# Block compression of a paged cache: four products per two blocks, or three

## The reference

```
def compress(kv, w1, w2, pe):
    c = kv[:, :n_chunk * CMP_STRIDE].reshape(B, n_chunk, CMP_STRIDE, 2, N_KV_HEADS, HEAD_DIM)
    lo = jnp.einsum('bnjchd,cjde->bnche', c, w1[:, :CMP_STRIDE])
    hi = jnp.einsum('bnjchd,cjde->bnche', c, w1[:, CMP_STRIDE:])
    pe_term = jnp.einsum('cjd,cjde->ce', pe, w1)
    pre = lo[:, :-1] + hi[:, 1:] + pe_term[:, None, :]
    return jnp.einsum('bnche,ced->bnchd', jax.nn.gelu(pre), w2)
```

## Time and profile before

| | us |
|---|---|
| median of 3 runs | 1815.0 (1814.69 to 1815.51) |
| the profiled execution | 1820.48 |
| its span | 1818.8 |
| granted clock of TensorE, mean | 0.992 |
| PE busy | 1761.8 (97%) |
| DVE busy | 1205.3 (66%) |
| POOL busy | 802.4 (44%) |
| ACT busy | 765.5 (42%) |
| DMA moved | 214.60 MB, mean 118 GB/s |

### The profile page before, as it was taken

One profiled execution on the slowest core, in us unless ns is written; L12 is line 12 of the kernel. 1 busy time (PEld: TensorE's weight loads), 2 busy tenths in 40 slices (PEclk: granted clock), 3 DMA queues, 4 the chain that ended last, 5 costly groups with the idle time before them and its releaser, 6 DMA issues.

```text
span 1818.8 us, 36969 instructions
## 1 busy us (share of the span) xinstructions
PE 1761.8 (97%) x14084; PEld 1641.3 (90%) x14084; DVE 1205.3 (66%) x1909; ACT 765.5 (42%) x1433; POOL 802.4 (44%) x763
## 2 busy tenths in 40 slices
PE   8999999999998999999999899999999999999998
PEld 7999998999995767676899899999999999999998
DVE  6789975675466676767746754554587879845535
ACT  5312333345345666666524333333343333314435
POOL 2203972224303434344444666656565555325531
PEclk9999999999998999999999999999999999999999
DMA  4321365446413444444313222323393732332214
GB/s 157 126 75 44 105 192 151 131 98 166 109 49 117 132 126 128 121 126 117 119 47 129 102 95 106 119 95 107 119 310 127 212 130 96 134 102 63 59 35 142
DMA packets 189983, 214.60 MB, mean 118 GB/s; under 512 B 23012, under 2 KB 152736, under 8 KB 189287
## 3 DMA queue, kind: packets, MB, share of 16 engines
q1 hardware_dynamic: 179357, 188.89, 33.8%
q0 software_dynamic: 7840, 21.25, 4.2%
q10 hardware_dynamic: 2610, 2.10, 0.4%
HBM read 181.22 MB, written 35.55 MB: 119 GB/s over the span
## 4 chain that ended last, share of the span: by engine, by line
PE 53%; DVE 8%; issue 3%; ACT 3%; POOL 2%; DMA 1%; ACTq 0%; SPq 0%; DVEq 0%; POOLq 0%
PE ps L2660 11%; PE ps L3043 7%; PE ps L2665 6%; PE ps L2420 4%; PE ps L3048 4%; PE ps L200 3%; PE ps L1827 3%; PE ps L1839 3%; PE ps L1815 3%; PE ps L3556 2%; PE ps L1866 2%; POOL S L1782 1%; PE ps L206 1%; DVE S L2076 1%; PE ps L3566 1%
## 5 line engine op out<-in xcount | busy, mean ns | idle before, releaser
L1782 POOL TENSOR_SCALAR S<-S,inv,gate_p 128x640 f32<-128x640 f32 (+7 forms) x186 | 124.3, 685 | 195.5 <-DVE inv L2086 195.5
L1166 DVE SCALAR_TENSOR_TENSOR y<-u,conv_w,y 128x1024 f32<-128x1024 f32 x120 | 156.5, 1350 | 1.2
L433 POOL DMA_DIRECT2D raw<-in_cache_cmp_kv_dram x124 | 77.8, 631 | 149.9 <-DVE relaid L1252 121.1
L1010 PE MATMUL ps_p<-Xhi,w1hi 128*128 128x256 f32 x544 | 139.3, 293 | 1.4 <-ACT Xhi L715 1.4
L3043 PE MATMUL ps<-dn_op_hi,dn_hi 128*128 128x264 f32 x672 | 136.6, 285 | 2.8 <-DVE dn_op_lo L3091 2.8
L3043 PE MATMUL ps<-dn_op_lo,dn_hi 128*128 128x264 f32 x672 | 135.7, 283 | 0.0
L1010 PE MATMUL ps_p<-Xlo,w1hi 128*128 128x256 f32 x544 | 132.8, 283 | 0.0
L1236 DVE TENSOR_TENSOR Xlo<-ps_p,Xhi 128x512 fp32r<-128x512 f32 x132 | 85.0, 684 | 59.1 <-ACT Xhi L715 58.9
L715 ACT ACTIVATE Xhi<-ps_p 128x512 fp32r<-128x512 f32 x132 | 72.4, 598 | 105.0 <-PE ps_p L935 97.6
L1963 ACT ACTIVATE S<-S,mn 128x64 f32<-128x64 f32 (+8 forms) x180 | 108.7, 608 | 2.1 <-DVE mn L2076 2.1
L2660 PE MATMUL ps<-s_hi,up_hi 128*128 128x264 f32 x512 | 104.8, 286 | 3.0 <-ACT rstd L2630 3.0
(11 more groups left out here) (502 smaller groups left out, 4922.1 us busy)
## 6 DMA issues: line engine op xcount, KB each, us to landing
s_raw<-in_cache_slc_kv_dram SPq DMA_DIRECT2D x256, 128.0 KB, 2.1
dn_op_raw<-hidden SPq DMA_DIRECT2D x21, 1056.0 KB, 6.0
raw<-in_cache_cmp_kv_dram SPq DMA_DIRECT2D x132, 128.0 KB, 4.2
hidden<-cs SPq DMA_DIRECT2D x32, 528.0 KB, 2.6
up_raw<-in_w_up_dram SPq DMA_DIRECT2D x16, 1024.0 KB, 5.5
raw<-in_cache_cmp_kv_dram POOLq DMA_DIRECT2D x124, 128.0 KB, 4.4
dn_w<-in_w_down_dram SPq DMA_DIRECT2D x48, 256.0 KB, 5.2
win_raw<-in_w_in_dram SPq DMA_DIRECT2D x38, 256.0 KB, 3.3
```

The lines of the kernel that those rows point to most:

```text
L433: eng.dma_start(raw[s][DH * half:DH * half + DH, i, :], page.rearrange("o q f -> (o q) f")).then_inc(raw_loaded[0 if g < 2 else part][s], 16)
L1010: mm = nc.tensor.matmul(ps_h[n % 2][:, 0:w], ws[cc][:, j, :], x[n % 2][:, j % 8, slice(j // 8, j // 8 + w)], start=(j == 0 and m == 0), st ...
L1166: i = V_.scalar_tensor_tensor(out=y, in0=x, scalar=w, in1=y, op0=ALU.mult, op1=ALU.add)
L1782: nc.gpsimd.tensor_scalar(x, x, inv[:, n % 3, 3 * e + br:3 * e + br + 1], c.gate_p[:, i, H * br + h:H * br + h + 1], ALU.mult, ALU.mult).t ...
```

## The change

Blocks 2m and 2m+1 are computed from chunks 2m, 2m+1 and 2m+2 with three products in place of four. With P0 = hi x chunk(2m), P1 = lo x chunk(2m+1) and P2 = (lo - hi) x (chunk(2m) - chunk(2m+1)), block 2m is P0 + P1 + P2 and block 2m+1 is P1 + P0 of the next pair of chunks. P0 and P1 are split in three fp32r products as before; P2 is one plain f32 product per token pair, of weights `w1diff` and columns `Xdiff`.

The unit becomes a pair (`CPAIRS`): keys or values with both heads, 18 in all, each of four steps (72 steps). A step covers two token pairs: 8 transposes into two banks, two copies on ACT (`Xdiff`, `Xhi`), two subtractions on DVE (`Xlo`, `Xdiff`), 12 fp32r and 2 f32 products of 256 columns on PE (68 columns for the prompt). `odd` on ACT copies P1 out, `combine` on DVE makes three additions per pair, `keep` moves from DVE to ACT. Each half chunk of 8 tokens is a row of 8 KB: a page is 16 rows in 16 partitions, a sequence's 32 pages fill one of two buffers `raw`. SP issues all pages; loading a sequence waits until the sequence two before is relaid, and that of sequence 0 until the projection's last tile is done and the gates are sent. The relay copies move from DVE to POOL, two per step. The position term is run through layer 1 as eight more rows of the prompt's buffer. Weight differences and low parts are made on DVE after the convolution; the second weight comes in one load. The layer norm, the swish and the tables are spread over other places of the same loops: a chunk of the norm has DVE's additions in step 0 of a pair, PE's sum in step 1 and DVE's centring in step 3, and in the same step 3 ACT waits for the centring and squares.

The diff, cut to its core; removed lines are left out, since they stand in the kernel above:

```diff
@@ -230,16 +230,19 @@
+CPAIRS = [(None, 0), (None, 1)] + [(b, cc) for b in range(B) for cc in range(2)]
+NPAIR = len(CPAIRS)
+NST = 4 * NPAIR
...
+    w1diff = [c.at("w1_difference0", [P, 8, P], F32, LATE_A), c.at("w1_difference1", [P, 8, P], F32, LATE_A + 24 * K1)]
+    raw = [c.at("raw0", [P, 4, HALF_T * 2 * KVH * DH], F32, U_OFF), c.at("raw1", [P, 4, HALF_T * 2 * KVH * DH], F32, PROJ_OFF + 512)]
+    NC = 2 * P
+    X_OFF = U_OFF + 32 * K1
+    Xhi = [c.at(f"Xhi{s}", [P, 4, 2 * P], F32R, X_OFF + 8192 * s) for s in range(2)]
+    Xlo = [c.at(f"Xlo{s}", [P, 4, 2 * P], F32R, X_OFF + 8192 * s + 4096) for s in range(2)]
+    odd_part = c.at("odd_part", [P, 2 * P], F32, X_OFF + 20480)
+    hid = c.at("hid", [P, 2, 2, NC], F32, WRAW_OFF)
...
+        def relay_of(st, h):
+
+            b, cc = CPAIRS[st // 4]
+            src, out = raw[1 if b is None else b % 2], relaid[st % 2]
+            if b is None:
+                src, out = src[:, 2:4, :], out[:, 0:2]
+            t = 2 * (st % 4)
+            src = src.rearrange("p g (t c h d) -> p g c h t d", t=HALF_T, c=2, h=KVH)[:, :, cc, h, t:t + 2, :]
+            return out[:, :, h, :].rearrange("p g (t d) -> p g t d", d=DH), src
 
@@ -475,6 +491,21 @@
             both_read(sp, "conv")
             sp.dma_start(a["prompt_conv"][0, 0], crow[SR - HIST:SR, 0, :]).then_inc(crow_sent, 16)
             sp.dma_start(a["sample_conv"][0, :, HIST - NEW:HIST, :], crow[:, 1, :]).then_inc(crow_sent, 16)
+            def load_pages(b):
+                if b == 0:
+                    sp.wait_ge(conv_step, conv_taps)
+                    sp.wait_ge(s_added, CW)
+                    sp.wait_ge(turned[1], aux("conv") + 1)
+                    sp.wait_ge(W.done, NT)
+                else:
+                    sp.wait_ge(relaid_ready, 8 * b)
+                for q in range(NPG // 4):
+                    _, at = nc.values_load_multi_w_load_instructions(
+                        c.pages[0:1, ds(b * NPG + 4 * q, 4)], engines=[mybir.EngineType.SP], min_val=0, max_val=N_POOL - 1)
+                    for k, page in enumerate(at):
+                        n = 4 * q + k
+                        sp.dma_start(raw[b % 2][16 * (n % 8):16 * (n % 8) + 16, n // 8, :], cs_rows[ds(page, 1)].rearrange("o x f -> (o x) f")).then_inc(raw_loaded[b % 2], 16)
+
             def spill_q(g):
                 t = TILES.index(("q", g))
                 sp.wait_ge(free[t % 2], t // 2 + 1)
...
                 sp.dma_start(g_dram[e].rearrange("g (b h t) -> h (g b) t", h=H, t=NEW),
                              gT[H * e:H * e + H, T:R].rearrange("h (b t) -> h b t", t=NEW)).then_inc(g_moved, 16)
+            load_pages(0)
             sp.wait_ge(g_moved, 48)
             for e in range(3):
                 sp.dma_start(c.gate_s[:, :, e], g_dram[e].rearrange("g p -> p g"), allow_slow_non_contiguous=True).then_inc(g_moved, 16)
+            sp.wait_ge(gate_turned, 1)
+            sp.wait_ge(q_out, 16 * PAIRS)
+            sp.wait_ge(qb_ready, 1)
+            for b in range(1, B):
+                load_pages(b)
+            sp.wait_ge(relaid_ready, 8 * B)
             sp.dma_start(c.q[:].rearrange("p g r -> p (g r)"), q_dram).then_inc(c.q_back, 16)
             sp.wait_ge(crow_sent, 32)
             sp.wait_ge(g_moved, 96)
...
+            def relay(st):
+                b, cc = CPAIRS[st // 4]
+                if st == 0:
+                    pool.wait_ge(alo_read, 1)
+                    pool.wait_ge(prompt_loaded, 48)
+                elif b is not None and cc == 0 and st % 4 == 0:
+                    pool.wait_ge(raw_loaded[b % 2], 16 * NPG * (b // 2 + 1))
+                if st >= 2:
+                    pool.wait_ge(chunks_turned, st - 1)
+                for h in range(KVH):
+                    out, src = relay_of(st, h)
+                    if b is None:
+                        nc.gpsimd.tensor_copy(out[:, 0:1], src[:, 0:1])
+                        i = nc.gpsimd.tensor_copy(out[0:8, 1:2], src[0:8, 1:2])
+                    else:
+                        i = nc.gpsimd.tensor_copy(out, src)
+                i.then_inc(relaid_ready, 1)
 
...
+            for st in range(NST):
+                n, s = divmod(st, 4)
+                relay(st)
...
+            def hi(st):
+                act.wait_ge(chunks_turned, st + 1)
+                if st == 0:
+                    act.wait_ge(W.done, NT)
+                after(act, used, st - 1)
+                nc.scalar.activation(split_columns(st, Xdiff[st % 2]), turned_columns(st)[:, 2:4], ACT.Copy)
+                nc.scalar.activation(split_columns(st, Xhi[st % 2]), turned_columns(st), ACT.Copy).then_inc(hi_ready, 1)
+
+            def odd(n):
+
+                act.wait_ge(used, 4 * n + 4)
+                after(act, combined, n)
+                w = n_columns(n)
+                src, out = [x.rearrange("p (h w) -> p h w", w=P)[:, :, 0:w] for x in (ps_h[n % 2][0][:, NC:2 * NC], odd_part)]
+                nc.scalar.activation(out, src, ACT.Copy).then_inc(odd_kept, 1)
+
...
             def gelu(n):
+                b, cc = CPAIRS[n]
+                act.wait_ge(combined, n + 1)
                 if b is None:
...
+            for st in range(1, NST):
+                n, s = divmod(st, 4)
+                if s == 2 and n:
+                    odd(n - 1)
+                hi(st)
...
+            def turn(st):
+                n = st // 4
+                if st >= 2:
+                    pe.wait_ge(lo_ready, st - 1)
+                    pe.wait_ge(diff_ready, st - 1)
+                elif st == 1:
+                    both_read(pe, "rows8")
+                else:
+                    pe.wait_ge(free[1], 9)
+                pe.wait_ge(relaid_ready, st + 1)
+                groups = ((0, P), (1, 8)) if CPAIRS[n][0] is None else ((0, P), (1, P), (2, P), (3, P))
+                for h in range(KVH):
+                    for g, rows in groups:
+                        mm = nc.tensor.transpose(ps_x[st % 2][:, h, P * g:P * g + rows], relaid[st % 2][0:rows, g, h, :], c.ident[0:rows, 0:rows])
+                mm.then_inc(chunks_turned, 1)
 
...
+            def layer1(st):
+                n, s = divmod(st, 4)
+                b, cc = CPAIRS[n]
+                w = n_columns(n)
+                v = st % 2
+                if s == 0:
...
+                    elif n == 1:
+                        pe.wait_ge(w1_lo, 3)
+                        pe.wait_ge(gate_kept, 1)
+                    else:
+                        pe.wait_ge(combined, n - 1)
+                        pe.wait_ge(l2_kept, n - 1)
+                    j, var = divmod(n - 1 - NORM_PAIR, 2)
+                    if 0 <= j < NCH:
+                        pe.wait_ge(ln_stat if var else ln_centred, j + 1)
+                pe.wait_ge(lo_ready, st + 1)
+                halves, difference = ps_h[n % 2]
+
+                def columns(x):
+                    return x.rearrange("p (h w) -> p h w", w=P)[:, :, 0:w]
+
+                for k, j in enumerate(token_pairs(st)):
+                    for e, at in ((0, j + 8), (1, j)):
+                        out = columns(halves[:, NC * e:NC * e + NC])
+                        first, last = s == 0 and k == 0 and e == 0, s == 3 and k == 1 and e == 1
+                        nc.tensor.matmul(out, w1hi[cc][:, at, :], columns(Xhi[v][:, 2 * e + k, :]), start=first, stop=False)
+                        nc.tensor.matmul(out, w1hi[cc][:, at, :], columns(Xlo[v][:, 2 * e + k, :]), start=False, stop=False)
+                        nc.tensor.matmul(out, w1lo[cc][:, at, :], columns(Xhi[v][:, 2 * e + k, :]), start=False, stop=last)
+                if s == 0 and n < 2:
+                    pe.wait_ge(d_made, n + 1)
+                pe.wait_ge(diff_ready, st + 1)
+                out = columns(difference[:, 0:NC])
+                for k, j in enumerate(token_pairs(st)):
+                    mm = nc.tensor.matmul(out, w1diff[cc][:, j, :], columns(Xdiff[v][:, k, :]), start=(s == 0 and k == 0), stop=(s == 3 and k == 1))
...
+            for st in range(NST - 2):
+                n, s = divmod(st, 4)
+                turn(st + 2)
+                layer1(st)
+                if st == 1:
...
+            def lo(st):
+                dve.wait_ge(hi_ready, st + 1)
+                V_.tensor_tensor(split_columns(st, Xlo[st % 2]), turned_columns(st), split_columns(st, Xhi[st % 2]).bitcast(F32), ALU.subtract).then_inc(lo_ready, 1)
+
+            def difference(st):
+                x = split_columns(st, Xdiff[st % 2])
+                V_.tensor_tensor(x, turned_columns(st)[:, 0:2], x, ALU.subtract).then_inc(diff_ready, 1)
+
+            def combine(n):
+
+                b, cc = CPAIRS[n]
+                halves, diff = ps_h[n % 2]
+                dve.wait_ge(odd_kept, n + 1)
+                after(dve, l2_done, n - 1)
+                out = hid[:, (n + 1) % 2].rearrange("p h (i e) -> p h i e", e=2)
                 if b is None:
+                    w = slice(0, 33)
```

(24 more changed lines are left out.)

618 lines of the change are left out of this document (244 added, 374 removed).

## The result

The changed kernel takes 1831.3 us (median of 4 runs, 1830.0 to 1836.8) beside 1815.3 us for the kernel before on the same chip: ratio 1.0085, 95% interval 1.0066 to 1.0104. It is 16 us slower. The profiled execution took 1832.4 us, span 1830.6, 11.9 us over that of before, which lay 5.5 us above its own median. The forecast was 1842.

The account below looks back on a forecast made before the run. Block compression was taken as bounded by PE's own work. First layer 1 at 309.4, plus 1.6, 231.0, 29.5 and 2, ends the stage at 573.5 against 546.7: +26.8 us, median 1842, range 1806 to 1888.

Parts of the forecast that it names:

- the likeliest case: Whole launch: SP's page issues set the period of a sequence; 1842 us, own range 1830 to 1856, chance 0.45.
- The start: Ahead of sequence 0: pages wait for the gates, start at 267.2, land by 304.1; layer 1 starts at 309.4.
- SP's queue: SP's page issues: 32 pages take 33.0 us a sequence (ends 28.7 and 33.0), more than compute's 29.5.
- rival 1: SP issues faster than compute, below 29.9 us a sequence, so the change gains: 1809 us, chance 0.21.
- The transfers: Page transfers into 16 partitions: 141 GB/s, 0.93 us a page, 30 us a sequence, just under SP's issue time.
- Rival 2: Narrow page transfers bound the sequences, from 127 GB/s down: 1904 us at 103 GB/s, chance 0.24.
- Compute: PE and the chain between engines in the cache sequences: 29.5 us a sequence alone, against 32.7 before.
- The norm's stalls: ACT's square waits for DVE's centring: some 3 us for each of three chunks.
- The clock: PE at half clock after each wait's end: 2 us in the sum, only the last sequence's counting.
- POOL's copies: POOL's two strided relay copies per step: 0.77 us each, 1.54 a step, costing nothing but at a sequence's start.
- Rival 3: POOL's strided copies bound the sequences, from 2.06 us each: 1885 us at 2.4; chance 0.10, shared with another late engine.
- The tail: Behind the last steps: first scores, query's return and last second layer stay there, nothing changes.

Follow-up runs that it names:

- early pages: Changed kernel with the first 16 pages of sequence 0 issued ahead of the gates: 1820.6 us, ratio 1.0031 to the kernel before.
- resident pages: Changed kernel loading pages for sequences 0 and 1 alone, the other six computing on old data: 1830.8 us, ratio 1.0088 to the kernel before.
- f1_three: Changed kernel with 16 pages issued ahead of the gates, prompt products of 128 columns and the norm's square one step later: 1813.1 us, ratio 0.9973.

## Why the prediction was right, and which of its steps was not

The sign, the place of the loss (a late start) and the range held. That page issues would also eat the gain in the middle did not come true, and that 1831 lies inside the likeliest case's own range, at its lower end, is partly luck, as the terms show:

- **The start** was right as a cause, and the time of its wait came out by luck. Pages begin at 267.05 (forecast 267.2) and are relaid from 302.76 on (last landing forecast 304.1); but SP was through at 292.9 and not at 300.2, and the last pages landed some 10 us behind it, not 3.9, with the DMA engines full. Two errors cancelled. The early pages show that this wait cost 10.6 us. PE's idle time was forecast as some 20 us around 285 to 309 and was 13, because six of the prompt's eight steps, at half clock, took 27 us where some 20 was forecast for all. "The prompt's steps ... are done before that" was wrong: two of them stood behind the wait, and layer 1 of sequence 0 began at 315.70, 6.3 us later than the forecast 309.4.
- **SP's queue** is the step that failed. "I take 33.0, the row of the same line": an issue cost 0.316 us, below both of my ends (0.333 and 0.469), and 32 pages went out in 25.8 us, so SP set no period behind the start; compute did, at 29.6 us. With that, rival 1's condition (under 29.9 us a sequence) was met and PE did not idle at every eighth step; that rival's 1809 us did not come about: layer 1 began 10.6 us later than its 305.1, and the norm and the tail added 4.2 and 4.0. The 0.469 us came from a row with 64 rows per issue, the 0.333 from one with 128; the number of rows named was no guide. Only with the destination's rows eight apart did 16 rows cost 0.496 us, and then SP set the period at 31.4 to 35.2 us.
- **The transfers** were sized right (141 GB/s forecast, 135 to 142 measured in stretches of 30 us from 303 to 483 at shares of 0.90 to 1.03, above the other figure of 104 that the forecast gives), though the way there, one factor applied twice, was a guess. They bound nothing but the start. Rival 2 fell with the resident pages, whose time is the same.
- **Compute** was right in size: 29.5 us a sequence forecast, 29.6 measured without the norm; eight sequences at 29.5 are 236, and 4.2 more for the norm are the 240.2 measured. Its parts were off in both directions: a difference product took 0.43 us, not 0.57, so PE is busy for 27.5 us in 30 and not throughout; the chain between engines is part of the rest, as the run with the shortened chain shows.
- **The norm's stalls** were right: 3 us each forecast, 3.4 measured, some 1.4 us of each reaching the end of a sequence, and moving the square gave 5.3 us. They were costed in the part on the chain, but not in the sum, where SP's 33.0 covered them.
- **The clock** was wrong: 2 us in the sum for half clock, when PE stood at 0.50 from 268 to 318 (idle for 13 us of it). I had looked only at waits as its cause; in the prompt the clock fell while PE was busy without a gap, on products of 68 columns where the kernel before had 256. Wider products brought the clock back earlier and 4.7 us.
- **POOL's copies** were 0.615 us each (0.77 forecast) and hidden, as forecast. Rival 3 fell.
- **The tail** was said not to change and grew by 4.0 us in the profiled executions. After the last layer-1 product (555.9) ACT copies the odd part (556.06), DVE combines until 557.53, and only then ACT applies the activation (557.73), where before it read PSUM at once (546.75): 2.0 us. The last second layer is eight products and not four: 0.45. The remaining 1.5 us, in which PE's own queue holds it, no run took apart.

So the forecast was 11 us too high from errors that went against each other. SP's bound (231 us for seven sequences where 29.5 each give 206.5) was 24.5 us too much, and the second gate transfer (1.6) and the half clock at the end (2) did not show. Against them stood the later first product (6.3), the norm (4.2) and the tail (4.0), which the sum lacked. That leaves 13.6 us, and with the 1.4 of the later stages the 15 between the forecast's span (1818.8 + 26.8 = 1845.6) and the measured 1830.6. Of the 16 us between the medians the profiled executions show 11.9; the difference is mostly that the profiled execution of before was itself 5.5 us above its median.

The change's own gain is there, 21 us from the first product of sequence 0 to the last of sequence 7, of the 25 that the forecast put on PE's arithmetic. f1_three shows what is left when the start is mended in part: its first product comes at 301.34 and its last layer 1 ends at 535.05, 27.5 us less than the kernel before needs for the same stretch, but it starts 15.8 us later and has the same longer tail. So only 0.27% of the launch is gained; what keeps the rest is the late start and the tail, not the sequences.

## What to carry to other kernels

Full DMA engines in a profile prove nothing by themselves: take the transfers away (compute on old data) and see whether the time moves. When products or transfers are cut at the head of a stage, look at what the first one waits for and at PE's clock there before counting what each later one saves. And when an order of data must be changed, put the stride on the PSUM side of an ACT or DVE instruction: in SBUF, a strided write or a strided moving operand cost nearly double here. And measure a stage between the same two events before and after: from the first product of a sequence to the last this change gains 21 us, in a kernel that as a whole loses 16.
